# A chunked recurrence with its inverses folded into the chunk matrices, two lines of inverses and one bank for a chunk's forms

## The chip, the cores and the metric

The kernel runs on one core of a Trainium2 chip. The metric is the time of one execution in microseconds (us), as the device measures it. A core has TensorE (matrix products), VectorE, ScalarE, GpSimd (elementwise work), SyncE (here it only starts transfers), an on-chip memory of 128 partitions and, for products, eight banks of accumulators with 512 fp32 columns each. Each engine takes its instructions in the order in which they were written; semaphores order the engines among each other. In the profile, PE is TensorE, DVE VectorE, ACT ScalarE, POOL GpSimd.

## The reference, cut to what matters

A two layer trunk on 1024 prompt frames and 8 streams of 16 sample frames, model width 1024, fp32. Layer 0 mixes tokens by a gated delta rule with 16 heads of 64, layer 1 by banded attention; each is followed by a SwiGLU block. The change touches the delta rule alone:

```python
def step(S, inp):
    r_t, w_t, k_t, v_t, na_t, b_t = inp
    sa = jnp.einsum('bhvk,bhk->bhv', S, na_t)
    S = S * w_t[:, :, None, :] + sa[..., None] * b_t[:, :, None, :] + v_t[..., None] * k_t[:, :, None, :]
    return S, jnp.einsum('bhvk,bhk->bhv', S, r_t)
s_final, out = lax.scan(step, s0.astype(f32), xs)
```

`S` is a head's 64 x 64 state. `na_t` is the negative normalised key, `b_t` that key times a gate, `w_t` the decay. Before it stand projections, decays and a key norm; behind it a norm of each head's output, a bonus term, a gate and the output projection.

## The kernel before, in words

The recurrence is a phase of its own, `recurrence_phase`. It treats the heads two at a time: `PAIRS` = 8 head pairs, one head in partitions 0 to 63, the other in 64 to 127. Time is cut into 18 chunks of 64 frames: 16 of the prompt, one after the other, and two that hold four sample streams each.

Within a chunk the rule is solved in matrix form. `form` computes the chunk's products of decayed keys, queries and values (the *forms*); masks make them triangular. The matrix `I - AB` of the chunk is inverted by doubling blocks: `x0` and `init` set up X and its transpose Y, and each of `LEVELS` levels has two half turns (`invert` with half 0 and 1), Q = L X and then X += Y Q, Y += Q Y. A *step* passes the state through a chunk: w = values + A S, then u = Y w, then S = decay (S + B u + K V), with the outputs beside it. So each of 16 steps goes three times from TensorE to VectorE and back: w (copy L1770), u (copy L1775), state (L1783). Every chunk's step needs the state of the one before.

Two helpers issue every such product as two 64 x 64 products, one for each head: `heads` (line 1309) reads and writes the same half of the partitions, `cross` (line 1315) writes the other half:

```python
def heads(out, lhsT, rhs, start=True, stop=True):
    for lo, hi in halves:
        last = pe.matmul(out[lo:hi], lhsT[lo:hi], ...)
def cross(out, lhsT, rhs, start=True, stop=True):
    for (lo, hi), (to, end) in zip(halves, halves[::-1]):
        last = pe.matmul(out[to:end], lhsT[lo:hi], ...)
```

The banks are FORM_D, FORM_C (forms by heads and by cross), MX, MY (inverses), WU, SB, OB (w and u, state, outputs) and one piece bank, which all other products of the phase share in turn.

What the order is: the work is a list of items for all engines, and each engine walks through it and does its part of each item. `PATTERN`, a string written by hand, merges five threads for each pair: A the serial steps of this pair, B forms, C the preparation of the next pair (sigmoids, the decay scan L1685 with a subtraction behind it, exponentials, key norm by `ksum` and `kexp`, `write`, bonus product), D the finish of the previous pair (`center`, `vsum`, `affine`, `gate`), E the inverses. Chunks are inverted in groups (`GROUPS`), all chunks of a group in one half turn. `stream` puts filler products where TensorE would stand idle, in the first pair's preparation and in the last pair.

## Time and profile before

| | |
|---|---|
| time, median of 3 runs | 3544.43 us (3542.29 to 3555.04) |
| profiled execution: span | 3544.3 us |
| profiled execution: time beside the span | 3544.3 us, core 0, the only core |
| TensorE busy | 3356.9 us, 95% |
| VectorE, ScalarE, GpSimd busy | 1734.0, 1350.6, 1688.5 us |
| mean granted TensorE clock | 0.990 of full |
| recurrence phase | about 411 to 1132 us |

Busy time is the union of an engine's instructions. A matmul's record spans its passage through the array, while the next one starts long before its end, so that a busy TensorE may still be waiting. An fp32 product leaves two records for each half, so a `heads` or a `cross` leaves four.

### The profile page before, as it was taken

What the parts mean: (1) busy time and instruction counts of PE and PEld (TensorE: products, weight loads), DVE (VectorE), ACT (ScalarE), POOL (GpSimd) and SP (SyncE); (2) the same over time, 40 slices, a digit from 0 to 9 for tenths busy, and PEclk for the clock granted to TensorE, in tenths of its full rate; (3) what the DMA queues carried; (4) which work ended last, traced back from release to release, by engine and by line L of the source; (5) the groups of instructions that cost most, each with busy time, mean ns of one, the idle gap of its engine ahead of it and who ended that gap; (6) DMA issues with size and microseconds to landing.
All of it is one profiled execution on the core that took longest, in us unless ns stands there. A gap on an engine that the chain in (4) does not pass through costs nothing. (4 is left out here: it accounts for less than half of the span.)

```text
span 3544.3 us, 86456 instructions
## 1 busy us (share of the span) xinstructions
PE 3356.9 (95%) x32975; PEld 2903.7 (82%) x32975; DVE 1734.0 (49%) x3390; ACT 1350.6 (38%) x2904; POOL 1688.5 (48%) x1513
## 2 busy tenths in 40 slices
PE   8999878888888999999999999999989999999999
PEld 7999767777776988888888887777769988888887
DVE  7113456777665374444444533333343744444444
ACT  6212444445543133333333434444453333333335
POOL 5434345555554445454554544344433354545455
PEclk9999999999999999999999999999999999999999
DMA  4422201111113111111111234544442111111111
GB/s 154 154 88 89 73 24 31 46 39 42 45 54 120 27 43 44 48 45 47 44 45 44 92 85 96 117 98 91 106 108 66 41 46 47 44 49 43 46 44 73
DMA packets 432738, 233.79 MB, mean 66 GB/s; under 512 B 190979, under 2 KB 417043, under 8 KB 431558
## 3 DMA queue, kind: packets, MB, share of 16 engines
q1 hardware_dynamic: 428882, 215.40, 21.7%
q10 hardware_dynamic: 3572, 14.33, 1.0%
q8 instruction: 211, 3.46, 0.4%
q14 instruction: 73, 0.60, 0.0%
HBM read 187.69 MB, written 47.21 MB: 66 GB/s over the span
## 5 line engine op out<-in xcount | busy, mean ns | idle before, releaser
L2615 DVE TENSOR_TENSOR H<-ps,H 128x512 f32<-128x512 f32 x608 | 419.3, 690 | 464.3 <-PE ps L2278 463.5
L2166 POOL TENSOR_TENSOR split<-work,split 128x512 fp32r<-128x512 f32 x280 | 379.5, 1361 | 495.0 <-ACT split L2437 487.9
L2278 PE MATMUL ps<-split,split 128*128 128x512 f32 x1824 | 514.0, 390 | 0.0
L2331 PE MATMUL ps<-xs,split 128*128 128x512 f32 x1920 | 512.5, 393 | 0.0
L1315 PE MATMUL ps<-arena 64*64 64x64 f32 (+2 forms) x8800 | 423.9, 236 | 50.1 <-DVE arena L1770 14.6
L2331 PEld LDWEIGHTS ps<-xs,split 128*128 128x128 f32 x1920 | 349.9, 188 | 68.1
L2278 PEld LDWEIGHTS ps<-split,split 128*128 128x128 f32 x1824 | 339.9, 188 | 70.9 <-DVE H L2615 0.7
L1315 PEld LDWEIGHTS ps<-arena 64*64 64x64 f32 x8800 | 319.7, 136 | 87.5 <-issue 38.2
L2331 PE MATMUL ps<-split,split 128*128 128x512 f32 x1440 | 366.1, 390 | 0.5 <-issue 0.5
L3205 PE MATMUL ps<-xs,split 128*128 128x384 f32 x1656 | 361.2, 355 | 2.6 <-POOL split L3119 2.6
L600 PE MATMUL ps<-mixed,wsplit_mix 128*128 128x384 f32 x1872 | 331.7, 339 | 7.6 <-DVE mixed L823 7.6
L600 PEld LDWEIGHTS ps<-mixed,wsplit_mix 128*128 128x128 f32 x1872 | 330.1, 189 | 8.9 <-DVE mixed L823 8.9
L1309 PE MATMUL ps<-arena 64*64 64x64 f32 (+2 forms) x5632 | 304.4, 241 | 27.4 <-DVE arena L1775 13.2
L2331 PEld LDWEIGHTS ps<-split,split 128*128 128x128 f32 x1440 | 267.6, 188 | 55.5 <-issue 1.0
L3205 PEld LDWEIGHTS ps<-xs,split 128*128 128x128 f32 x1656 | 277.9, 189 | 30.1 <-issue 22.4
L1309 PEld LDWEIGHTS ps<-arena 64*64 64x64 f32 x5632 | 245.8, 135 | 60.7 <-DVE arena L1775 27.3
L2437 ACT CAST split<-work 128x512 fp32r<-128x512 f32 x280 | 174.1, 622 | 138.1 <-PE ps L2331 107.7
L2171 POOL TENSOR_TENSOR split<-work,split 128x256 fp32r<-128x256 f32 x168 | 132.7, 790 | 172.9 <-ACT split L2444 170.3
L3368 ACT ACTIVATE work<-work,work 128x640 f32<-128x640 f32 (+3 forms) x144 | 101.0, 702 | 257.3 <-DVE work L3459 249.3
L3171 POOL TENSOR_SCALAR work<-work,work 128x640 f32<-128x640 f32 (+2 forms) x64 | 95.0, 1484 | 188.7 <-DVE work L3464 188.7
L1284 POOL TENSOR_TENSOR arena<-arena 128x320 f32<-128x320 f32 (+2 forms) x144 | 123.6, 866 | 127.0 <-PE ps L1315 100.0
L2475 ACT COPY ps<-ps 128x512 f32<-128x512 f32 x120 | 68.8, 574 | 281.0 <-PE ps L2331 281.0
(328 smaller groups left out, 5875.4 us busy)
## 6 DMA issues: line engine op xcount, KB each, us to landing
work<-in_ffn_w_gu SPq DMA_DIRECT2D x168, 256.0 KB, 2.9
work<-in_ffn_w_down SPq DMA_DIRECT2D x168, 128.0 KB, 2.4
...
work<-in_cache_k SPq DMA_DIRECT2D x256, 64.0 KB, 2.2
...
```

The lines of the kernel that those rows point to most:

```text
L600: last = pe.matmul(mem.ps[:, 4 * v + c, 0:CW], mem.wsplit[:, v, w, k * P:(k + 1) * P], mixed[part][:, k, c * CW:(c + 1) * CW], start=(k == ...
L1284: pool.tensor_tensor(m.lt[:, n % 2, 0:G, :], m.at[:, slot_of(pr, g), 0:G, 0:64], spread(m.level[:, l, :], G), ALU.mult).then_inc(lt_ready, 1)
L1309: last = pe.matmul(out[lo:hi], lhsT[lo:hi], rhs[lo:hi] if rhs is not None else eye(lo, hi), start=start, stop=stop)
L1315: last = pe.matmul(out[to:end], lhsT[lo:hi], rhs[lo:hi] if rhs is not None else eye(lo, hi), start=start, stop=stop)
L2166: pool.tensor_tensor(w[1], frm, w[0].bitcast(F32), ALU.subtract).then_inc(u_lo, 1)
L2171: pool.tensor_tensor(w[1], mem.down_raw, w[0].bitcast(F32), ALU.subtract).then_inc(d_lo, 1)
L2278: last = pe.matmul(full(DOWN + j % 2), w[part][:, (m % 2) * P:(m % 2 + 1) * P], mem.hid[xpart][:, SEG[h]], start=(a == 0), stop=(a == 2))
L2331: last = pe.matmul(full(to), unit(i)[part][:, k * P:(k + 1) * P], operand[xpart][:, k, :], start=(first and k == 0 and a == 0), stop=(k == ...
L2437: act.copy(w[0], w[2] if i == 3 else mem.raw[:, RAW_OF[i], :]).then_inc(u_hi, 1)
L2615: dve.tensor_tensor(at, full(DOWN + j % 2), at, ALU.add).then_inc(added, 1)
L3205: last = pe.matmul(ps[:, GEMM + b, 0:CW], mem.wsplit[:, (3 * p + u) % 2, w, k * P:(k + 1) * P], mem.xs[:, part, k, c * CW:(c + 1) * CW], s ...
L3368: act.activation(pr, pr, ACT.Exp, scale=-1.0, bias=mem.mx[:, N % 2, h:h + 1], accum_out=mem.rsum[:, N % 2, h:h + 1]).then_inc(ex_ready, 1)
```

## The change

The inverse no longer acts on w within a step. Once a group's inverse is done, a new item `fold` multiplies it into two of the chunk's forms (BR, which gives outputs, and BT, which gives the state's update), so that a step has two turns: w, and the state. For that, Y starts from the transposed form instead of being turned by a product (`init` goes, `x0` on GpSimd sets up both), and X and Y lie side by side so that VectorE adds to both by one operation. All products of the inverses are `heads` now. The forms of a chunk lie in one bank, 512 columns, all by `cross`; two such banks alternate, VectorE masks 320 columns in one operation and ScalarE copies 192. Groups are four chunks each, in two independent lines (threads E and F), each with a bank. Outputs are collected eight chunks at a time. The order has a new string for the start and a new pattern. The filler products in the last pair's steps go. Lines of the changed kernel: `heads` is 1311, `cross` 1317.

```diff
-GROUPS = [(0, 5), (5, 5), (10, 6), (16, 2)]
+GROUPS = [(0, 4), (4, 4), (8, 4), (12, 4), (16, 2)]
+ROUNDS = [(0, 8), (8, 8), (16, 2)]
...
-LEVELS = [5, 5, 5, 3]
-NL = sum(LEVELS)
+LEVELS = [5, 5, 5, 5, 3]
+LINE = [0, 1, 0, 1, 0]
...
-PATTERN = ("EABACDEAAEACAEABECBAEDBAECABAEDAEBCEACEACAEAACAAEECAEDEABEADAECACEACACABEADECAEADECAEAACEDEAEBAEABAEABAEABEAEA"
-           "BACEADEAECADAEACEACAAABAEAAEABCAABAAEAAECCBEAEBAECA")
...
+FIRST = (
+    "CCCCCCCCCCCCCCCCCCCCCEBBBBBBBBEBEBEFFEFEFCEBFEBFEBFEBFEBFEBFFCFC")
+PATTERN = (
+    "DEAEACCFABEAFCEAFACECAFEADAFCAECAFCCDEFADCCEDFCADECAFEADFAABAECFCACDEACDEACBEABCEFABEABEACAEBCAEBACBAEBCAEBAEA"
+    "DEFAFAABEABFEABFEAABFEBAAFAEAFAEAFCEBFEAAFAFABF")
...
-        out += [("x0", o, g), ("init", o, g)] + [("invert", o, (g, l, half)) for l in range(1, LEVELS[g] + 1) for half in range(2)]
...
+            out += [("x0", o, g)] + [("invert", o, (g, l, half)) for l in range(1, LEVELS[g] + 1) for half in range(2)] + [("fold", o, g)]
...
-        FORM_D, FORM_C, MX, MY, WU, SB, OB, PIECE = range(8)
+        FORM, M, WU, SB, OB, PIECE = (0, 1), (2, 3), 4, 5, 6, 7
...
+                    for a, part in enumerate((AB, BA)):
+                        chain.link(pool.tensor_tensor(xy[:, :, a, :], m.slots[:, c0:c0 + G, part], spread(m.level[:, 0, :], G), ALU.mult))
+                    pool.tensor_tensor(xy.rearrange("p q a c -> p (q a) c"), xy.rearrange("p q a c -> p (q a) c"), spread(m.eye, 2 * G), ALU.add).then_inc(x_ready[line], 1)
...
-                    heads(fd[:, 0:192], m.bb[:, e, n, :], m.ar[:, e, n, :])
-                    cross(fc[:, 0:192], m.kb[:, e, n, :], m.ar[:, e, n, :])
-                    heads(fd[:, 192:256], m.ar[:, e, n, 64:128], m.bb[:, e, n, :]).then_inc(formed_d, 1)
-                    cross(fc[:, 192:256], m.vb[:, e, n, :], None).then_inc(formed, 1)
...
+                    fb = bank[:, FORM[now % 2], :]
+                    cross(fb[:, 0:128], m.kb[:, e, n, :], m.ar[:, e, n, :])
+                    cross(fb[:, AB], m.ar[:, e, n, 0:64], m.bb[:, e, n, :])
+                    cross(fb[:, 192:320], m.bb[:, e, n, :], m.ar[:, e, n, :])
+                    cross(fb[:, BT], m.bb[:, e, n, :], None)
+                    cross(fb[:, KT], m.kb[:, e, n, :], None)
+                    cross(fb[:, VT], m.vb[:, e, n, :], None).then_inc(formed, 1)
...
-                            last = cross(bank[:, MX, q * 64:(q + 1) * 64], m.lt[:, n % 2, q, :], m.x[:, q, :])
...
+                            last = heads(mb[:, q * 64:(q + 1) * 64], m.lt[:, line, n % 2, q, :], xy[:, q, 0:64])
...
+                            last = heads(mb[:, q * 128:q * 128 + 64], xy[:, q, 64:128], qs[:, q, :])
                             if l < LEVELS[g]:
-                                last = cross(bank[:, MX, q * 64:(q + 1) * 64], m.y[:, gb, q, :], m.q[:, q, :])
-                                if q == G - 1:
-                                    last.then_inc(m2_done, 1)
-                            last = heads(bank[:, MY, q * 64:(q + 1) * 64], m.q[:, q, :], m.y[:, gb, q, :])
-                        last.then_inc(m3_done, 1)
+                                last = heads(mb[:, q * 128 + 64:q * 128 + 128], qs[:, q, :], xy[:, q, 64:128])
+                        last.then_inc(m2_done[line], 1)
...
+                    for q in range(G):
+                        last = heads(bank[:, M[line], q * 128:(q + 1) * 128], m.xy[:, line, q, 0:64], m.slots[:, c0 + q, 256:384])
...
-                            cross(bank[:, WU, 0:64], m.ar[:, e, n, 64:128], S, False, True).then_inc(w_done, 1)
-                            state_values(pr, g, q)
-                    elif part == 1:
-                        if q == 0:
-                            outs(pr, g, 0)
+                            cross(bank[:, WU, 0:64], m.ar[:, e, n, 0:64], m.s[:, n % 2, :], False, True).then_inc(w_done, 1)
+                            state_values(n)
+                            if not first_out(n):
+                                read(pr, n)
+                    else:
+                        if n == GROUPS[g][0]:
+                            pe.wait_ge(fold_ready[LINE[g]], folds_before(pr, g) + 1)
                         pe.wait_ge(w_ready, now + 1)
-                        if q == 0:
-                            pe.wait_ge(y_ready, turns_before(pr, g) + LEVELS[g] + 1)
-                        cross(bank[:, WU, 64:128], m.y[:, gb, q, :], m.w).then_inc(u_done, 1)
-                        if q + 1 < G:
-                            outs(pr, *after)
-                    else:
-                        pe.wait_ge(u_ready, now + 1)
-                        ob = bank[:, OB, q * 64:(q + 1) * 64]
-                        pe.wait_ge(state_values_done, 16 * pr + n + 1)
-                        heads(bank[:, SB, 0:64], tm[:, 0:64], m.u, False, True).then_inc(s_done, 1)
-                        pe.wait_ge(outs_done, now + (2 if q + 1 < G else 1))
-                        last = cross(ob, m.u, at[:, 64:128], False, False)
+                        cross(bank[:, SB, 0:64], m.slots[:, n, BT], m.w, False, True).then_inc(s_done, 1)
+                        if first_out(n):
+                            outs(pr, n)
+                            if n:
+                                read(pr, n)
                         if n:
-                            last = cross(ob, S, m.ar[:, e, n, 128:192], False, q == G - 1)
-                        last.then_inc(serial_done, 1)
-                        w_values(pr, *after)
+                            pe.wait_ge(read_done, 15 * pr + n)
+                        heads(out_of(n), m.w, m.slots[:, n, BR], False, last_out(n)).then_inc(serial_done, 1)
+                        w_values(pr, n + 1)
+                        if not last_out(n):
+                            outs(pr, n + 1)
...
-                    act.copy(tm[:, 64:192].rearrange("p (x c) -> p x c", c=64),
-                             bank[:, FORM_C, 0:256].rearrange("p (x c) -> p x c", c=64)[:, 0:4:3, :]).then_inc(tmc_ready, 1)
-                    act.wait_ge(atd_ready, now + 1)
-                    act.copy(tm[:, 0:64], bank[:, FORM_D, 0:64]).then_inc(tm_ready, 1)
+                    act.wait_ge(at_ready, now + 1)
+                    act.copy(m.slots[:, n, 320:512], bank[:, FORM[now % 2], 320:512]).then_inc(tm_ready, 1)
...
+                    act.copy(m.slots[:, c0:c0 + G, 256:384], bank[:, M[line], 0:G * 128].rearrange("p (q c) -> p q c", q=G)).then_inc(fold_ready[line], 1)
...
-                    dve.tensor_tensor(at[:, 0:192], bank[:, FORM_D, 64:256], mask[:, 0:192], ALU.mult).then_inc(atd_ready, 1)
-                    dve.wait_ge(tmc_ready, now + 1)
-                    dve.tensor_tensor(at[:, 192:320], bank[:, FORM_C, 64:192], mask[:, 192:320], ALU.mult).then_inc(at_ready, 1)
...
+                    dve.tensor_tensor(m.slots[:, n, 0:320], bank[:, FORM[now % 2], 0:320], mask, ALU.mult).then_inc(at_ready, 1)
...
-                        dve.tensor_tensor(m.x[:, 0:G, :], wide(MX), m.x[:, 0:G, :], ALU.add).then_inc(x_ready, 1)
-                    dve.wait_ge(m3_done, n + 1)
-                    dve.wait_ge(y_ready, turns_before(pr, g) + l)
-                    dve.tensor_tensor(m.y[:, gb, 0:G, :], wide(MY), m.y[:, gb, 0:G, :], ALU.add).then_inc(y_ready, 1)
...
+                    dve.tensor_tensor(xy, bank[:, M[line], 0:G * 128].rearrange("p (q c) -> p q c", q=G)[:, :, 0:xy.shape[2]], xy, ALU.add).then_inc(x_ready[line], 1)
...
-                        dve.tensor_copy(m.u, bank[:, WU, 64:128]).then_inc(u_ready, 1)
+                        dve.tensor_copy(m.w, bank[:, WU, 0:64]).then_inc(w_ready, 1)
...
-            STREAMED_LAST = {("sw", 0): 2, ("su", 0): 2, ("sw", 1): 2, ("su", 1): 2, ("center", 0): 3, ("ns", 1): 4, ("vsum", None): 4}
+            STREAMED_LAST = {("center", 0): 3, ("ns", 1): 4, ("vsum", None): 4}
...
-                    stream(2 if what == "step" and arg[0] == NG - 2 and arg[1] >= 3 else STREAMED_LAST.get((what, arg), 0))
+                    stream(STREAMED_LAST.get((what, arg), 0))
```

How the instructions move, in TensorE's order. First two pieces of one pair's stretch before: head sums (L1321), a second half turn of a group of six where every other product is a `cross` (L1315) and a `heads` (L1309), and a chunk's forms with 192 and 64 columns.

```order
L1321 MATMUL ps<-headones,arena 128x56 x9
L1315 MATMUL ps<-arena 64x64 x2
L1309 MATMUL ps<-arena 64x64 x2
L1315 MATMUL ps<-arena 64x64 x2
L1309 MATMUL ps<-arena 64x64 x2
...
L1309 MATMUL ps<-arena 64x192 x2
L1315 MATMUL ps<-arena 64x192 x2
L1309 MATMUL ps<-arena 64x64 x2
L1315 MATMUL ps<-ident,arena 64x64 x2
```

The same kind of place after: a stretch behind the head sums, with half turns that are `heads` (L1311) alone, sixteen and thirty in a row, then a chunk's forms by `cross` (L1317) alone, and a fold of 128 columns for four chunks.

```order
L1323 MATMUL ps<-headones,arena 128x56 x9
L1330 MATMUL ps<-ident,arena 128x128 x3
L1311 MATMUL ps<-arena 64x64 x16
L1330 MATMUL ps<-ident,arena 128x128 x3
...
L1317 MATMUL ps<-arena 64x128 x2
L1317 MATMUL ps<-arena 64x64 x2
L1317 MATMUL ps<-arena 64x128 x2
L1317 MATMUL ps<-ident,arena 64x64 x6
L1311 MATMUL ps<-arena 64x128 x8
```

The pairs of the two kinds no longer alternate, neither in the inverses nor in the forms. Second, VectorE before, around the decay scan (L1685, printed as the operation that carries it) of one pair: copies of w and u (L1770, L1775), the state (L1783), sums of the inverses (L1757, L1760), masks (L1745, L1747).

```order
L1775 COPY arena<-ps 128x64
L1783 SCALAR_TENSOR_TENSOR arena<-ps,arena 128x64
L1685 SCALAR_TENSOR_TENSOR arena<-arena 128x1152
L1687 TENSOR_TENSOR arena<-arena 128x1152
L1770 COPY arena<-ps 128x64
L1721 TENSOR_SCALAR arena<-ps 128x18
L1723 RECIPROCAL arena<-arena 128x18
L1757 TENSOR_TENSOR arena<-ps,arena 128x384
L1760 TENSOR_TENSOR arena<-ps,arena 128x384
L1775 COPY arena<-ps 128x64
```

And after, the same place: scan (L1670), one sum for X and Y (L1733), the w copy (L1743) and the state (L1751), the key norm (L1679) and the finish of the previous pair (L1705 to L1712).

```order
L1743 COPY arena<-ps 128x64
L1674 TENSOR_SCALAR arena<-ps 128x18
L1676 RECIPROCAL arena<-arena 128x18
L1670 SCALAR_TENSOR_TENSOR arena<-arena 128x1152
L1672 TENSOR_TENSOR arena<-arena 128x1152
L1733 TENSOR_TENSOR arena<-ps,arena 128x512
L1751 SCALAR_TENSOR_TENSOR arena<-ps,arena 128x64
L1705 TENSOR_SCALAR arena<-ps 128x18
L1707 RECIPROCAL arena<-arena 128x18
L1679 SCALAR_TENSOR_TENSOR arena<-arena,vec,ps 128x384
L1733 TENSOR_TENSOR arena<-ps,arena 128x512
```

A sum of an inverse and the state's update now stand behind the scan where a w copy stood; between two of a step's operations there is a sum of the inverses more often than not.

## Rows read from the trace of the kernel before

**Rows 1.** The page: span, busy time, and VectorE's costliest group.

```profile
span 3544.3 us, 86456 instructions
PE 3356.9 (95%) x32975; PEld 2903.7 (82%) x32975; DVE 1734.0 (49%) x3390; ACT 1350.6 (38%) x2904; POOL 1688.5 (48%) x1513
...
L2615 DVE TENSOR_TENSOR H<-ps,H 128x512 f32<-128x512 f32 x608 | 419.3, 690 | 464.3 <-PE ps L2278 463.5
```

**Rows 2.** Windows of the phase, cut at decay scans; busy us of each engine.

```profile
core 0: us, PE busy (x) PEld busy (x) DVE busy (x) ACT busy (x) POOL busy (x), PEclk, DMA share, GB/s
...
448.00:499.50 51.50, 39.75 (x1070) 34.32 (x1069) 21.48 (x68) 19.73 (x58) 21.61 (x27) 0.83 0.09 26
499.50:581.00 81.50, 66.78 (x2091) 57.09 (x2091) 51.57 (x146) 38.97 (x104) 43.27 (x48) 0.96 0.12 33
581.00:905.00 324.00, 287.74 (x8472) 239.92 (x8472) 230.49 (x617) 160.45 (x420) 176.90 (x188) 1.00 0.15 42
905.00:988.30 83.30, 72.64 (x2118) 60.45 (x2118) 57.18 (x154) 40.12 (x105) 44.20 (x47) 1.00 0.14 41
988.30:1132.00 143.70, 124.36 (x3189) 98.06 (x3187) 89.64 (x236) 59.65 (x146) 61.69 (x62) 0.99 0.19 61
```

**Rows 3.** Timeline of TensorE: start, duration of the run, records.

```profile
581.39 0.90 PE L1315 MATMUL ps<-ident,arena 64*64 64x64 f32 x24
```

**Rows 4.** The same timeline, a second half turn of six chunks.

```profile
585.52 0.23 PE L1315 MATMUL ps<-arena 64*64 64x64 f32 x2
585.54 0.23 PE L1309 MATMUL ps<-arena 64*64 64x64 f32 x2
...
585.99 0.22 PE L1315 MATMUL ps<-arena 64*64 64x64 f32 x2
586.00 0.23 PE L1309 MATMUL ps<-arena 64*64 64x64 f32 x2
```

**Rows 5.** Groups by line, 581 to 905 us: TensorE's 64-column products, idle before, releasers.

```profile
L1315 PE MATMUL ps<-arena 64*64 64x64 f32 x3904 | 167.3, 223 | 21.8 <-DVE arena L1770 7.8 <-DVE arena L1757 3.7 <-issue 3.4
...
L1309 PE MATMUL ps<-arena 64*64 64x64 f32 x2496 | 124.2, 225 | 9.3 <-DVE arena L1775 6.2 <-ACT arena L1622 2.9
```

**Rows 6.** Timeline of TensorE at the forms of a chunk.

```profile
623.47 0.38 PE L1315 MATMUL ps<-arena 64*64 64x192 f32 x2
...
623.55 0.36 PE L1309 MATMUL ps<-arena 64*64 64x192 f32 x2
```

**Rows 7.** Groups by line and shape, 581 to 905 us: busy, mean ns of one, idle before.

```profile
L1745 DVE TENSOR_TENSOR arena<-ps,arena 128x192 f32<-128x192 f32 x72 | 25.6, 355 | 20.7 <-PE ps L1309 18.9
...
L1747 DVE TENSOR_TENSOR arena<-ps,arena 128x128 f32<-128x128 f32 x72 | 20.8, 289 | 2.5 <-ACT arena L1614 1.5
...
L1622 ACT COPY arena<-ps 128x320 f32<-128x320 f32 x40 | 17.1, 427 | 23.1 <-PE ps L1315 22.1
L1783 DVE SCALAR_TENSOR_TENSOR arena<-ps,arena 128x64 f32<-128x64 f32 x60 | 16.7, 279 | 10.0 <-PE ps L1309 9.0 <-DVE arena L1732 0.9
L1757 DVE TENSOR_TENSOR arena<-ps,arena 128x320 f32<-128x320 f32 x32 | 15.6, 488 | 7.0 <-PE ps L1315 7.0
...
L1770 DVE COPY arena<-ps 128x64 f32<-128x64 f32 x64 | 14.0, 219 | 11.4 <-PE ps L1315 9.7 <-PE ps L1309 1.2
...
L1605 ACT ACTIVATE arena<-ps 128x384 f32<-128x384 f32 x12 | 5.8, 487 | 7.6 <-PE ps L1315 7.6
...
L1598 ACT ACT_TABLE_LOAD x4 | 5.1, 1283 | 10.0 <-DVE arena L1691 10.0
...
L1598 ACT ACTIVATE arena<-arena 128x1152 f32<-128x1152 f32 x4 | 4.6, 1162 | 0.0
```

**Rows 8.** Timeline of VectorE at the decay scan of a pair.

```profile
581.68 2.55 DVE L1685 TENSOR_TENSOR_SCAN arena<-arena 128x1152 f32<-128x1152 f32 x1
584.26 1.97 DVE L1687 TENSOR_TENSOR arena<-arena 128x1152 f32<-128x1152 f32 x1
```

**Rows 9.** Timeline of VectorE at the first two chunks' forms.

```profile
449.46 0.36 DVE L1745 TENSOR_TENSOR arena<-ps,arena 128x192 f32<-128x192 f32 x1 [0.21 <-DVE arena L1716]
...
451.43 0.36 DVE L1745 TENSOR_TENSOR arena<-ps,arena 128x192 f32<-128x192 f32 x1 [1.41 <-PE ps L1309]
```

369 lines of the change are left out of this document (163 added, 206 removed).

## The prediction

> **What bounds the kernel now.** I read the page's shares and busy digits first, then the windows of the recurrence phase, then TensorE's pace inside it, then who ends its waits. The page gives TensorE 95% of a span of 3544.3 us and the others at most 49% [rows 1]; outside the recurrence the change touches nothing, so 3544.3 minus that phase stays as it is. The profiled execution's span is 3544.3 us and the median of the three runs 3544.43 us, so the sum is made against either.
>
> The windows cut the phase, 411 to 1132 us, at the decay scans of its eight head pairs, one a pair. Four periods from the scan at 581 to that at 905 take 324 us, 81.0 us each, with TensorE shown busy for 287.7 of it, 71.9 a period, VectorE 57.6, ScalarE 40, GpSimd 44 [rows 2]. No engine but TensorE is near full, and TensorE shows 9 us of idle in a period. That understates it. A product's record is shown for 0.22 us, while the next may start in the same place 0.058 us later (below), so each turn that TensorE waits for hides some 0.16 us of waiting under the last record before it. With some 55 such turns in a period that is 9 us more. So I count 18 us of waiting and 63 us of product issue.
>
> The pace matters most here. Each logical fp32 product of 64 columns leaves two records. Where cross products stand alone, 24 records take 0.90 us including the 0.22 us tail: 28 ns a record, 0.117 us for a cross (two halves, four records) [rows 3]. In a half turn of the inverses, where cross and heads alternate, L1315 pairs start at 585.52 and, eight pairs on, at 585.99: steps of 0.059 us, each with two cross and two heads records: 0.117 us for a cross and a heads together [rows 4]. So alternation makes the second product free. The Trainium skill (TensorEngine Tiling (Array Packing), Key Properties) says that the four 64x64 tiles work independently; the heads products use two of them and the cross products the other two. The trace agrees with it: 0.059 us for four records against 0.117.
>
> TensorE's own waits name VectorE's copies L1770 and L1775 (w and u of a step), its sum L1757 and ScalarE's copy L1622 (both of the inverses) [rows 5]. These are turns that the change removes, or puts more work behind.
>
> **The change part by part**, for one period; a unit is 0.117 us, 64 columns by one kind of product.
>
> *Forms, 18 a period.* Before, heads and cross of 192 and of 64 columns overlap: 4 units (a heads of 192 starts 0.08 us after a cross of 192 [rows 6]). After, all eight blocks go by cross into one bank: 8 units. Added 18 x 4 x 0.117 = 8.4 us.
>
> *Inverses.* The first half turns cost 86 units before and after (16 chunks by 5 levels, 2 by 3). The second half turns but the last have 16 x 4 + 2 x 2 = 68 chunk levels; each had cross and heads overlapped (1 unit), now two heads (2 units): added 8.0 us. The turned start (18 units) goes, the fold (18 x 2 units) comes: added 2.1 us.
>
> *Steps.* The u product goes: 8 products a step become 7, minus 16 units. But before, seven of eight stood so that a heads lay beside a cross, and now three heads follow each other (output, next w, next output): I count about 105 units of issue before and 113 after. Added 0.9 us.
>
> *Seams.* Where a cross item stands beside a heads item, one unit overlaps. The new order has about 40 such seams more than counted above: minus 4.7 us. The rest of a period (gates, sums, root expansions, samples: about 20 us) is the same work. Sum: 8.4 + 8.0 + 2.1 + 0.9 - 4.7 = 14.7 us; issue rises from 63 to 77.7 us, and the whole phase's by about 117 us.
>
> *What comes back is waiting.* A turn of a step is the product's 0.22 us, 0.05 to VectorE, 0.21 for the copy and 0.05 back: 0.53 us, and 0.60 us with the state's 0.28 us operation [rows 7]. There were three turns for each of 16 steps and now two. In the new order each of the two has an inverse half turn or more behind it (0.47 us for 4 chunks, 0.94 us for a second half), plus 0.3 us of the step's own products, so nearly all are covered. The inverses ran in one line: 18 levels of about 3.2 us (two half turns of 0.7 us, copy 0.43, sum 0.49, four handovers [rows 7]) plus starts, 70 of 81 us, nearly a bound of its own. Two lines have 13 and 10 levels of the same length, 42 and 32 us: no bound. Forms had one pair of banks, and VectorE's 0.36 and 0.29 us with a copy of ScalarE between stood between two of them; now two banks alternate.
>
> *What remains.* VectorE saves 355 + 289 ns against about 490 ns (the 320-wide sum) for each form, 2.8 us, and the u copies, 3.7 us, and about 1 us in the inverses (a 512-wide sum is 0.69 us by the page's L2615 [rows 1], where there were two of about 0.48). It is not the bound, so this pays only through waits. But its long operations stay in one queue: scan 2.55, subtraction 1.97 [rows 8]. At the scan, the new order puts center, two inverse halves and a step after the head sums, and the second head sums must wait for ScalarE's root of the first (table load 1.28 and 1.16 us [rows 7]) and then center's two reads, the square 0.49 us and a copy as long: those end about 6.1 us after the first sums start, and TensorE has 4.3 us of work. 1.9 us of wait. The expansions behind them alternate in one bank: 0.6. Later halves stand behind ScalarE's exponentials: 0.5. The 1152-wide product for the bonus (as long as the subtraction, 1.97) and the gates: 1. The other places: 2. Sum about 6 us a period. Below, 2 us (the piled work hides all but the scan); above, 12 us, two thirds of what there is now. I take 6, the places counted.
>
> So a period comes to 77.7 + 6 = 83.7 us, 2.7 more than 81.0, and over the six periods from the scan at 499.5 to that at 988.3: the first has less to do (no finish of a pair before it) and idles most now (66.8 busy of 81.5 [rows 2]): 8 us less issue than the others, so 69.5 + 7 of waits = 76.5, minus 5; the other five, now 81.5 on average (407.3 for five [rows 2]), plus 11.5.
>
> *The ends.* 448 to 499.5 us: the first forms are now 2.0 us apart (449.46, 451.43 [rows 9]), waiting on that chain; with two banks they come at about 1.06. Issue there is 44 us after, plus 4 of waits: 48 against 51.5, minus 3.5. The tail, 988.3 to 1132 us, takes 143.7 us for 106 us of issue, 38 us of waiting, the last steps having nothing behind them. After, 120.5 us of issue; 5 us of waits up to its steps, 4 in them (two turns instead of three), 7 in the finish: 137, minus 7. The removed filler products (26 in the last pair) are issued where TensorE waits anyway and count nothing; were that cover gone, each costs 0.15 us, 4 us in all. The copy of the identity blocks at the start, one VectorE instruction, likewise.
>
> Sum: -5 + 11.5 - 3.5 - 7 = -4 us: 3540 us.
>
> The rows of VectorE show a fixed part: 64 wide 0.22, 192 wide 0.36 us [rows 7]. The Trainium skill (VectorE: DVE Perf Modes, The TRN2 errata) says that such operations pay a fixed extra time each, so that fewer and longer ones are cheaper; by it alone VectorE's 7.5 us a period would come off. The trace puts VectorE 23 us from full.
>
> **The rivals.**
> - *Faster: the waits all but vanish.* If only 2 us stay in a period, it is 79.7 us: 4 us less in six periods, and about 3 less at the ends: 3540 - 27 = 3513 us. For it: every turn named in [rows 5] gets more work behind it. Against: VectorE's long operations stay. It holds from waits under about 3.5 us. Chance 0.28.
> - *Slower: the in-order queues keep TensorE waiting while the products cost more.* Place: from the scan to the fold some 20 us later, where ScalarE holds two roots, a table load and three exponentials, each about as long as a root, in front of an inverse's copy, and VectorE the 4.5 us of the scan. If 11 us of waits stay, a period is 88.7: 5 us more by 6, and 2 at the ends: 3572 us. It decides from 9 us on. Against: both lines have work, so one may be late. Chance 0.28.
> - *Faster still: VectorE's saved time comes off in full,* as if its fixed cost for each operation bounded the phase: 8 x 7.5 = 60 us, 3484 us. Against it: VectorE's 23 us of idle in a period [rows 2]. Chance 0.02.
> - *The change does not do what it says:* the two turn step gains nothing, since steps were covered already and only forms and inverses gave waits. Then 2 more turns' waits stay, 3 us a period: 3558 us. This is inside my case; the same chance covers it.
>
> **How the numbers follow.** No change: 0.42, faster 0.30 (0.28 and 0.02), slower 0.28, where 0.5% (18 us) is about what a measurement of this kernel can tell from no change. The range leaves out the 0.02 and the ends: 3505 us is waits of 2 us with issue 1 us a period lower than counted, 3588 us is waits of 12 us (3578) with seams that give 1.2 us less in each of eight periods.
>
> **What would show it.** Right: TensorE's busy share in a period rises from 0.89 to 0.93 or more, while its products' issue takes 77 us; four steady scans stand 83 to 84 us apart; hardly any wait of TensorE ends with the w copy or the state's update; VectorE falls to about 50 us a period; the tail is 7 us shorter. Wrong: if heads alone run at 0.058 us, the added 14.7 us is not there and the kernel gains over 100 us; if scans stand 88 us apart, the queues hold it.

## The result, and the profile after

The changed kernel takes 3584.95 us (median of 4 runs, 3578.57 to 3595.91), the kernel before 3546.06 us, measured beside it (3542.29 to 3555.04): ratio 1.0114, 95% interval 1.009 to 1.0138. It is slower, by 39 us, where I forecast 3540 us and most likely no change. The time lies in my range (3505 to 3588 us), near its upper end, where I had put the rival with the in-order queues. The profiled execution has a span of 3594.0 us, 49.7 more than before. It is the longest of the four runs (3595.91 us), 11 us above the median, so a period read from it may be up to 1.5 us longer than usual; its mean granted clock, 0.982, is also the lowest of the four (the others have 0.984 to 0.987). Where that matters I give the medians' figure too.

The page of the changed kernel, to be held against [rows 1]: TensorE is busy for 91 us more, VectorE for 41 us less, and the span is longer. The two costliest groups of this phase are both products of 64 columns.

```profile
span 3594.0 us, 87138 instructions
...
PE 3448.1 (96%) x33525; PEld 3010.3 (84%) x33525; DVE 1693.0 (47%) x3045; ACT 1338.1 (37%) x2800; POOL 1759.1 (49%) x1633
...
q8 instruction: 214, 3.51, 0.4%
...
L1311 PE MATMUL ps<-arena 64*64 64x64 f32 (+1 forms) x9984 | 400.0, 228 | 17.8 <-issue 10.2
...
L1317 PE MATMUL ps<-arena 64*64 64x64 f32 (+4 forms) x4448 | 287.9, 252 | 14.4 <-DVE arena L1743 5.5
```

The windows of the phase in the changed kernel, cut at its decay scans as in [rows 2]; the columns are the length, then each engine's busy time with its instructions, the granted clock of TensorE, the DMA share and GB/s.

```profile
core 0: us, PE busy (x) PEld busy (x) DVE busy (x) ACT busy (x) POOL busy (x), PEclk, DMA share, GB/s
...
446.00:502.20 56.20, 50.23 (x1374) 45.60 (x1376) 28.43 (x57) 19.03 (x48) 36.65 (x48) 1.00 0.09 24
502.20:584.90 82.70, 74.15 (x2143) 67.75 (x2141) 46.76 (x101) 36.59 (x89) 52.89 (x62) 0.96 0.12 33
584.90:673.90 89.00, 83.04 (x2194) 73.03 (x2198) 52.73 (x113) 38.59 (x92) 53.15 (x62) 0.96 0.13 38
...
855.20:944.10 88.90, 83.21 (x2194) 73.34 (x2194) 52.66 (x113) 38.58 (x92) 53.08 (x62) 0.96 0.13 38
944.10:1033.00 88.90, 83.06 (x2194) 73.16 (x2195) 52.30 (x112) 38.52 (x92) 53.22 (x62) 0.96 0.13 38
```

The steady scans stand 89 us apart and not 81, and TensorE is busy for 0.93 of a period, where it was 0.89: busier, and later. By the scans of both traces: from the first scan to the second 68.6 us against 71.5, the first period 82.7 against 80.9, the next five together 448.1 against 407.5, the tail from the last scan to the end of the phase's products 143.6 against 142.5. So +40.6 of the 49.7 us lie in the five steady periods. The rest is -2.9, +1.8 and +1.1 us, and 9 us outside (the first scan 4.4 us later, the program behind the phase 4.8 us longer), which scatters between executions.

Which waits of TensorE are left, the list of waits from the scan at 673.9 to that at 1033.0 (four periods): in total, times, longest.

```profile
engine line waited for: us in total, times, longest us
PE ps L1323 <- ACT arena L1598: 6.5, 4, 1.6
PE ps L1311 <- issue: 6.2, 8, 1.7
PE ps L1317 <- DVE arena L1743: 2.5, 9, 0.4
PE ps L1317 <- DVE arena L1674: 1.4, 5, 0.3
PE ps L1311 <- DVE arena L1762: 1.3, 4, 0.4
```

The turns of the steps that ended TensorE's waits in [rows 5] have all but gone (L1743, the w copy, 0.6 us a period). The wait before the second head sums is there as forecast, 1.6 us by this list once a period, behind center's read L1598. The second row is what I had not thought of: TensorE stands and waits for nothing that the profile shows.

**Two ledgers.** To compare kernels I split a period in two. I added up, from the start times of TensorE's records over the last four periods, how far each start lies beyond the pace of the record before it (0.058 us for 64 columns, in proportion for more, 0.115 for a full-array product; only where it is more than 0.06 us beyond). "Gaps" are these sums a period, split by what the trace says ended them: a semaphore; the switch between full-array and quarter tiles; nothing, over or under 0.3 us. "Products" is the rest of the period, so a product that the half clock stretches (below) is mostly counted there. By it the 18 + 63 us of the prediction are 17.0 + 64.6.

```
kernel               period  products  gaps | semaphore  switch  nothing, long  nothing, short
before                81.5     64.6    17.0 |   11.9       1.7       1.6            1.8
both taken apart      82.8     68.6    14.2 |   10.2       1.7       1.0            1.3
before + products     90.3     71.1    19.3 |   11.7       5.0       1.1            1.5
before + cover        84.4     67.7    16.8 |   10.4       1.7       3.0            1.6
before, waits once    80.9     63.9    17.0 |   11.7       1.7       1.8            1.8
after                 89.8     75.4    14.4 |    7.1       1.7       2.5            3.1
after + filler        86.9     75.6    11.2 |    6.3       1.3       1.8            1.8
after, merged         89.2     69.9    19.3 |   10.5       1.7       3.7            3.4
after + products      97.1     82.7    14.4 |    7.2       4.8       0.1            2.3
after, slow copy      89.5     75.3    14.2 |    7.0       1.8       2.4            3.0
after, split          92.3     80.1    12.2 |    7.5       1.3       1.4            2.0
after + 216 waits     95.0     76.9    18.1 |    7.0       1.7       5.6            3.7
after without y       83.6     67.8    15.8 |    9.2       1.8       1.9            2.8
after, waits once     85.1     73.3    11.7 |    7.7       1.4       0.5            2.1
  with the filler    84.9     74.3    10.6 |    6.7       1.3       0.9            1.8
```

### The profile page after: what moved, and what is told of

It is laid out like the page before. It is cut to its first block and busy times, and to the rows that moved or that the text cites. A ratio compares the mean times of both kernels' runs of the same rounds, so it can differ in the third digit from the quotient of the medians.

```text
span 3594.0 us, 87138 instructions
## 1 busy us (share of the span) xinstructions
PE 3448.1 (96%) x33525; PEld 3010.3 (84%) x33525; DVE 1693.0 (47%) x3045; ACT 1338.1 (37%) x2800; POOL 1759.1 (49%) x1633
## 3 DMA queue, kind: packets, MB, share of 16 engines
q10 hardware_dynamic: 3572, 14.33, 1.0%
q8 instruction: 214, 3.51, 0.4%
## 5 line engine op out<-in xcount | busy, mean ns | idle before, releaser
L1311 PE MATMUL ps<-arena 64*64 64x64 f32 (+1 forms) x9984 | 400.0, 228 | 17.8 <-issue 10.2
L1311 PEld LDWEIGHTS ps<-arena 64*64 64x64 f32 x9984 | 351.8, 137 | 46.9 <-issue 31.2
L1317 PE MATMUL ps<-arena 64*64 64x64 f32 (+4 forms) x4448 | 287.9, 252 | 14.4 <-DVE arena L1743 5.5
L1317 PEld LDWEIGHTS ps<-arena 64*64 64x64 f32 x4448 | 198.6, 135 | 46.1 <-issue 21.0
L95 POOL TENSOR_SCALAR wsplit_mix<-stage_mix 128x1024 fp32r<-128x1024 f32 x26 | 76.1, 2926 | 202.6 <-PE ps L601 171.4
L2438 ACT COPY ps<-ps 128x512 f32<-128x512 f32 x120 | 68.8, 573 | 280.9 <-PE ps L2294 280.9
```

Of the source, the lines that this page charges most:

```text
L1311: last = pe.matmul(out[lo:hi], lhsT[lo:hi], rhs[lo:hi] if rhs is not None else eye(lo, hi), start=start, stop=stop)
L1317: last = pe.matmul(out[to:end], lhsT[lo:hi], rhs[lo:hi] if rhs is not None else eye(lo, hi), start=start, stop=stop)
```

## The experiments

Ratios are to the kernel before, with their 95% interval.

### Is the pace of alternated products what it was priced at?

**e1_turns_apart**: the kernel before, with the second half turn's cross products all ahead of its heads.

```
                         for q in range(G):
                             if l < LEVELS[g]:
                                 last = cross(bank[:, MX, ...], m.y[:, gb, q, :], m.q[:, q, :])
                                 ...
+                        for q in range(G):
                             last = heads(bank[:, MY, ...], m.q[:, q, :], m.y[:, gb, q, :])
```

> The kernel before with one edit: in a second half turn all cross products come first and all heads products after them, instead of one after the other. Same work, same waits. If products of one kind alone take 0.117 us for 64 columns and alternated ones 0.117 us for both (the pace theory), 68 chunk levels a period get 0.117 us longer, 8.0 us, 64 us over eight pairs, of which waits take up to a third: 3585 to 3610 us. If the kinds do not matter, or waits alone set the period (the queue theory), 3545 us, within 8.

3554.77 us, 1.0014 (1.0001 to 1.0026): between the two expectations.

**e2_forms_apart**: the kernel before, with the forms in the order heads, heads, cross, cross.

```
-                    cross(fc[:, 0:192], m.kb[:, e, n, :], m.ar[:, e, n, :])
                     heads(fd[:, 192:256], m.ar[:, e, n, 64:128], m.bb[:, e, n, :]).then_inc(formed_d, 1)
+                    cross(fc[:, 0:192], m.kb[:, e, n, :], m.ar[:, e, n, :])
```

> The kernel before with one edit: a chunk's forms as two heads products and then two cross products, instead of alternated. Pace theory: 4 units of 0.117 us more for each of 18 chunks, 8.4 us a period, 67 us in all, of which the waits between forms take part: 3565 to 3610 us. Queue theory: 3545 us, within 8.

3550.11 us, 1.0007 (0.9995 to 1.0019): no difference, against the pace that I had priced. **e3_both_apart**, both edits:

> The kernel before with both edits. Pace theory: the two add up, 16.4 us of issue a period, about what the change adds (14.7), without its shorter chain: 3620 to 3670 us, slower than the changed kernel's 3585. Queue theory: 3545 us, within 10.

3558.69 us, 1.0029 (1.0012 to 1.0046). In my sum the second half turns taken apart were worth 8.0 us a period and the forms 8.4. The products' ledger rises by 3.7 us in e1, by 0.5 in e2 and by 4.0 in e3: a run of one kind still overlaps the run or the item of the other kind that stands next to it. Gaps fall by 2.8 in e3, so that 1.2 us a period are left, 9 us in all. Both edits also move a semaphore forward (`m2_done` now stands ahead of the heads products, `formed_d` ahead of the first cross), so that VectorE can start earlier; the ratios alone therefore don't price the pace, the ledger does. The other way round, in the changed kernel:

**a3_merged**: a chunk's forms (cross) and the inverse half turn or fold (heads) that stands beside them are issued in turn, in 14 of 18 chunks; **a4_merged_center** is this with a1, below.

```
+                    a, b = form_calls(form[1], form[2]), line_calls(*inv)
+                    ca = cb = 0
+                    while a or b:
+                        if a and (not b or ca <= cb):
+                            cost, call = a.pop(0)
+                            ca += cost
+                        else:
+                            cost, call = b.pop(0)
+                            cb += cost
+                        call()
```

> The changed kernel with one edit on TensorE alone: where a chunk's forms (cross) stand next to a half turn or a fold (heads), 14 of 18 chunks, their products are issued alternately. Same products, same results, other engines as before. Pace theory: 4 to 8 units of 0.117 us overlap each time, 9 to 10 us of issue a period less; part becomes waiting, since each of the two also waits for the other's inputs: 3510 to 3550 us. Queue theory (waits set the period): 3580 us or more.

> Both: products of forms and inverses alternated, and the last center item early. Pace theory with the clock: the gains add, 3470 to 3520 us, faster than both kernels. Queue theory: not faster than the better of the two alone.

3586.01 us, 1.0100 (1.0083 to 1.0117), and 3600.96 us, 1.0146 (1.0129 to 1.0163), where the changed kernel has 1.0114. No gain clear of the scatter, and a4 is slower. The ledger says why: in a3, alternation takes 5.5 us of products off a period, and the gaps take 4.9 back, 3.4 on semaphores and 1.2 as long stalls that end on nothing. So in neither kernel is alternation worth its price in the period.

### The clock and the wait ahead of the head sums

In the profiled execution of the changed kernel the granted clock falls to half for 6.8 us in every period; before it did so in none of the steady ones. Windows of the changed kernel just ahead of a fall, and over it:

```profile
945.40:947.60 2.20, 0.61 (x25) 0.47 (x22) 2.17 (x2) 2.19 (x5) 2.20 (x1) 1.00 0.00 0
948.40:955.20 6.80, 6.53 (x59) 5.58 (x60) 3.35 (x8) 3.67 (x4) 2.98 (x1) 0.50 0.01 2
```

TensorE does next to nothing for 2 us (the wait behind L1598), then issues head sums, and the clock goes from 2.4 to 1.2 GHz 0.8 us after the first of them. The same wait doesn't always bring the fall: b4_after_split and d3_after_once (below) have it in each steady period, 1.83 and 1.74 us long, and their clock falls in only one and two of the last four.

**a1_center_early** reads the centers further ahead, **a2_filler** lets TensorE do filler products there in all pairs but the last.

```
-    "DEAEACCFABEAFCEAFACECAFEADAFCAECAFCCDEFADCCEDFCADECAFEADFAABAECFCACDEACDEACBEABCEFABEABEACAEBCAEBACBAEBCAEBAEA"
+    "DEAEACCFABEAFCEAFACECAFEADAFCAECAFDCCEFADCCEDFCADECAFEADFAABAECFCACDEACDEACBEABCEFABEABEACAEBCAEBACBAEBCAEBAEA"
```

```
+                if pr + 1 < PAIRS:
+                    fill({("vsum", None): 10, ("affine", 0): 3}.get((what, arg), 0))
```

> The changed kernel with one letter moved in its pattern: the last center item of the previous pair stands before the head sums and the scan instead of behind them, so that ScalarE reads it before the root and not after. The wait of TensorE before the second head sums (1.8 us) should go, and with it the drop of the clock: 4 to 5 us a period, 3550 us. Rival: ScalarE's queue holds the next thing instead (a copy of the inverses), the wait moves and the clock still falls: 3575 to 3585 us.

> The changed kernel with 10 filler products ahead of the second head sums and 3 ahead of the first root expansion in all pairs but the last, where TensorE waits; nothing else changes. Clock theory: the trace of the changed kernel shows the half clock for 6.8 us at each pair's scan, where TensorE waited 1.8 us, and none in the steady periods before; with the waits filled the clock stays up and each period is 2.5 to 3.4 us shorter: 3560 to 3568 us. If the drop has another reason (the low width of the head sums), or costs nothing since engines wait there anyway: 3585 us, within 8.

a1: 3590.72 us, 1.0114 (1.0097 to 1.013), periods of 89.6 us: the wait moves to other places, and the clock is still half for 6.0 us a period. a2: 3577.90 us, 1.0089 (1.0069 to 1.0109). First the window over four periods of the changed kernel, then that of a2:

```profile
673.90:1033.00 359.10, 334.26 (x8764) 293.70 (x8765) 210.03 (x445) 154.31 (x368) 212.54 (x248) 0.96 0.13 38
```

```profile
669.40:1017.00 347.60, 328.69 (x8817) 287.90 (x8821) 211.11 (x446) 154.37 (x368) 213.05 (x248) 1.00 0.14 39
```

With the clock held at 1.00, a period is 86.9 us: 2.9 us less in these four periods, of the 8.2 that the change adds. That is the forecast size, but by the medians the filler is worth only 7 us for the whole kernel, 1 us a period, where I expected 17 to 25, and the intervals of the two ratios overlap. The three other executions of the changed kernel had a higher clock than the profiled one already, so they had less to win. At least 5.3 us a period remain.

### What a period is made of: load tests

Is it the sum of the products, or a chain through VectorE, ScalarE and GpSimd? **b1_after_load** and **b2_before_load** put three filler products of 256 bf16 columns ahead of each chunk's forms in the six middle pairs, **b3_after_slow_q** lets ScalarE copy an inverse's first product chunk by chunk, **b4_after_split** halves the transposing products.

```
+                    fill(fb[:, 0:256], 3 if 0 < pr < PAIRS - 1 else 0)
                     cross(fb[:, 0:128], m.kb[:, e, n, :], m.ar[:, e, n, :])
```

```
-                    act.copy(m.q[:, line, 0:G, :], by64(bank[:, M[line], 0:G * 64])).then_inc(q_ready[line], 1)
+                    for q in range(G):
+                        last = act.copy(m.q[:, line, q, :], bank[:, M[line], q * 64:(q + 1) * 64])
+                    last.then_inc(q_ready[line], 1)
```

```
+                for c in (0, 32):
+                    for (lo, hi), (to, end) in zip(halves, halves[::-1]):
+                        last = pe.matmul(out[to:end, c:c + 32], lhsT[lo:hi], mem.ident[lo:hi, lo + c:lo + c + 32], start=True, stop=True)
```

> The changed kernel with three extra 256-column bf16 products of 128 rows ahead of each chunk's forms, in the six middle pairs: 54 products a pair. By the 28 ns that a 64-column record takes when the queue is dense, 256 columns are 0.11 us, so 5.8 us of TensorE work more in each of six periods, 35 us in all. Theory A (TensorE's issue sets the 88.9 us period, the product term of the forecast): periods grow by 5 to 6 us and the median by about 33 us, 3618. Theory B (a chain of waits through VectorE, ScalarE and GpSimd sets it, and TensorE has slack that sits in front of waits): periods grow by less than 3 us, the median under 15 us, below 3600.

> The kernel before with the same 54 extra 256-column products a pair in the six middle pairs (5.8 us a period). With TensorE waiting 16 us a period there, theory B says that most of it is absorbed in front of waits: under 3 us a period, median under 3565. If every product is paid in full, the period grows by 5 to 6 us and the median is about 3583: then even in the kernel before TensorE work adds to the period one for one, although it waits.

> The changed kernel with ScalarE copying the first product of an inverse turn chunk by chunk (four 64-column copies of 0.21 us, 0.86 us, in place of one of 0.37 us): each turn's chain longer by 0.48 us, ScalarE 10 us busier in a period (from 38.5 to 49). Nothing changes for TensorE. Theory A (issue of products): period within 1 us, median within 8 us of the changed kernel's. Theory B (the chain through the turns, queues in order): 13 turns of the longer line by 0.48 us are 6 us a period if that line is the chain, so a period of 92 to 95 and a median of about 3615 to 3630.

> The changed kernel with the three transposing products of a chunk's forms split into two of 32 columns each: the same columns, 6 products and 6 weight loads more a chunk, 216 records a period more on TensorE's queue (4516 to 4732). Theory C (instruction supply, 256 instructions in 3.4 to 4.1 us at least, 13 to 16 ns each, holds TensorE): 3 us a period, about 22 us in all eight, median about 3607. If columns alone count: same as the changed kernel within 5 us. If a record has a least time of its own near 28 ns whatever its width: 108 pairs a period by 28 to 56 ns less the columns saved, also 3 us; the two are told apart by stalls that end on nothing in the trace at each 256th instruction.

b1: 3633.04 us, 1.0236 (1.0216 to 1.0255). b2: 3597.85 us, 1.0129 (1.0112 to 1.0146). b3: 3585.70 us, 1.0091 (1.0073 to 1.0108). b4: 3622.65 us, 1.0205 (1.0186 to 1.0224). b1 and b2 came out above even the expectation that every product is paid, b3 where the theory of issue has it, and b4 15 us above its 3607 us, which had counted the added products and left out their weight loads.

The products are paid in both kernels, and more than in full: 7.3 us a period in the changed kernel and 8.8 in the one before, for 5.8 us of columns. (b2's profiled execution is 6 us above its median; by the medians, over six pairs, it is 8.0 and 7.8.) Timeline of TensorE in b1 at one of the places:

```profile
903.61 0.57 PE L1311 MATMUL ps<-arena 64*64 64x64 f32 x14
904.11 0.50 PE L1373 MATMUL ps<-ones 128*128 128x256 bf16 x3
904.54 0.43 PE L1317 MATMUL ps<-arena 64*64 64x128 f32 x4
```

The last pair of L1311 starts at 903.96, the next product of quarters at 904.54: 0.58 us where 0.058 would do, 0.52 for 0.33 us of columns. The rest is the switch to the full array and back. By the Trainium skill (TensorEngine Tiling (Array Packing), Key Properties) changing the tiling mode drains TensorE; the trace agrees, at 0.19 us for the two changes.

What does not react is as telling. The semaphore gaps stay: 11.9 and 11.7 us before, 7.1 and 7.2 after. They are round trips between items that stand close together in TensorE's order, and work elsewhere in the order covers nothing of them. The long stalls on nothing do react: they go from 2.5 to 0.1 us a period in b1, which the section on waits for nothing explains. And b3's chain, longer by 0.19 us in each of 23 turns (four copies take 0.56 us by the trace, not the 0.86 that I had expected), changes the period by 0.3 us or less. So a chain through the lines of inverses doesn't set it; that theory is out for additions of this size. b4's 216 product records more, with as many weight loads, cost 2.5 us a period: 4.7 us of products, with 2.2 us of gaps gone. But its clock stayed up in three of these four periods (half for 1.7 us a period, against 6.8), which hides part of the cost; by the medians it is 4.7 us. Its stalls on nothing did not grow, so it doesn't tell the supply of instructions from a record's own time.

**c1_before_cover** puts products directly ahead of a wait, **c3_after_no_y** takes products away.

```
+                        cover(q, SB, 64, True)
                         pe.wait_ge(w_ready, now + 1)
```

```
-                            if l < LEVELS[g]:
-                                last = heads(mb[:, q * 128 + 64:q * 128 + 128], qs[:, q, :], xy[:, q, 64:128])
```

> The kernel before with two extra 64-column products of two quadrants each directly ahead of TensorE's wait for the copy of w, in 13 steps of each of the six middle pairs: 0.117 us each, 0.23 us a step, 3.0 us a period, 18 us in all. Where the products stood elsewhere (ahead of the forms) every one was paid in full although TensorE waits 12 us a period on semaphores. If waits are short round trips, each covered only by what stands between its two ends, these products take the place of the wait (0.19 us each, 2.5 us a period): the period grows by less than 1 us and the median by less than 7 us. If waits don't depend on what stands ahead of them (VectorE's own queue sets when the copy comes), 3 us a period and 18 us.

> The changed kernel with the second product of the second half turn left out (the transposed inverse is not carried on; this leaves out part of the computation) and VectorE adding 64 columns a chunk in place of 128. 64 chunk-turns for the four prompt groups and 4 for the samples have it, 68 by 0.117 us = 8.0 us a period. If the sum of products sets the period: 89.6 to about 82, median about 64 us lower (some 3520). If the chain of a line or the waits set it, the period falls by less than 3 us.

c1: 3562.41 us, 1.0043 (1.0029 to 1.0058): periods 2.9 us longer (2.2 by the medians) for 3.0 us of products. The wait did give way, 1.5 us of semaphore gap a period, but 1.4 us came back as long stalls on nothing. Neither expectation held; the next section has the reason. c3 no longer carries the transposed inverse on, so it leaves out part of the computation and only measures what that part costs. 3540.03 us, 0.9974 (0.996 to 0.9987): 6.2 us a period less for 8.0 us of products (7.6 by the ledger, 1.4 given back in gaps); I had expected nearly all of the 8.0 and some 3520 us. The added products are a true cost: without this one part of them the changed kernel's time is 0.3% under the time before.

### Who ends a wait for nothing

The long stalls of TensorE that end on nothing, first in a3_merged, then in c1_before_cover (timeline, the idle time in brackets):

```profile
811.01 0.33 PE L1331 MATMUL ps<-arena 64*64 64x64 f32 x2 [1.25 <-issue]
...
815.11 0.27 PE L1331 MATMUL ps<-arena 64*64 64x64 f32 x2 [0.60 <-issue]
...
819.01 0.27 PE L1331 MATMUL ps<-arena 64*64 64x64 f32 x2 [0.71 <-issue]
```

```profile
736.86 0.32 PE L1315 MATMUL ps<-arena 64*64 64x64 f32 x2 [0.45 <-issue]
...
741.57 0.39 PE L1315 MATMUL ps<-arena 64*64 64x64 f32 x6 [0.81 <-issue]
...
746.33 0.45 PE L1315 MATMUL ps<-arena 64*64 64x64 f32 x9 [0.86 <-issue]
```

They come 3.9 to 4.8 us apart. I counted all records on TensorE's queue from the program's start: products, weight loads, and also the waits, register and branch instructions (with products and weight loads alone the remainders scatter). Of all steps over 0.45 us between two products that end on nothing, in the five periods from the third scan to the eighth, these stand at a record whose number leaves 165 to 167 when divided by 256:

```
before 8 of 8; after 14 of 14; a3_merged 19 of 19; c1_before_cover 23 of 23; a2_filler 14 of 14;
b4_after_split 8 of 8; c3_after_no_y 11 of 11; e3_both_apart 8 of 8; b3_after_slow_q 16 of 16
```

The same place modulo 256 in kernels with different programs: instructions reach TensorE in blocks of 256, and where it runs faster than blocks come, it stands at the block's edge. The queue q8 moves instructions, 16.4 KB a packet (the page of the changed kernel above: 214 packets, 3.51 MB). Its packets over four periods, in the changed kernel and in the one before:

```profile
q8 instruction: 70, 1.15, 1.3%
```

```profile
q8 instruction: 69, 1.13, 1.4%
```

TensorE's queue has 18064 and 17616 records there, which is 70.6 and 68.8 times 256; in b4_after_split and c3_after_no_y, with more and fewer instructions, it is 77 packets for 77.3 blocks and 62 for 62.1. In these four runs no two packets start less than 3.3 us apart, and the 14 stalls of the changed kernel all end 2.1 to 2.8 us after a packet's start. It fits that b1's fillers, long in columns and few in instructions, leave almost none of the long stalls. To measure the supply by itself:

**d1_dense_runs** puts in two long runs of products that wait for nothing, ahead of the second head sums.

```
+                    if pr in (2, 4):
+                        run(*((128, ("heads", "cross")) if pr == 2 else (256, ("heads",))), pb)
```

> The changed kernel with two long runs of 64-column fp32 products that wait for nothing, ahead of the second head sums: in the third pair 128 times heads and cross in turn (512 products), in the fifth pair 256 times heads alone (512 products); each product is two records with their weight loads, 2048 instructions a run. If the array alone sets the pace (0.117 us a step, both kinds in one step): 15 us for the alternated run, 30 us for heads alone. If the supply of instructions in blocks of 256 is a floor of 4.1 to 4.4 us a block (as between the stalls seen), both runs take 33 to 35 us after the first blocks, with stalls at every 256th instruction, and the alternated pace that the forecast priced holds only for as many instructions as are there in advance.

3641.15 us, 1.0256 (1.0238 to 1.0274). Timeline of TensorE at the alternated run, and at that of heads alone:

```profile
764.59 2.98 PE L1375 MATMUL ps<-ident 64*64 64x64 f32 x186 [1.62 <-ACT arena L1608]
768.72 2.10 PE L1375 MATMUL ps<-ident 64*64 64x64 f32 x128 [1.15 <-issue]
772.20 2.10 PE L1375 MATMUL ps<-ident 64*64 64x64 f32 x128 [1.38 <-issue]
775.95 1.26 PE L1375 MATMUL ps<-ident 64*64 64x64 f32 x69 [1.66 <-issue]
...
967.17 30.08 PE L1375 MATMUL ps<-ident 64*64 64x64 f32 x1024 [1.61 <-ACT arena L1608]
```

The alternated run does a block of 128 product records and as many weight loads in 2 us and then stands. From the stall at 768.72 to the one at 791.52 there are six blocks in 22.8 us: 3.80 us a block, 14.8 ns an instruction. The seven packets of q8 in these microseconds are all that the core's transfers show there, 3.5 to 4.0 us apart, and each stall ends 2.2 to 2.6 us after one starts. The run takes 28.1 us, not 15. Its mean granted clock is 0.94, but the clock was low almost only while the sixth block ran (3.33 us instead of 2.10), and the next block still came 3.76 us after it: the clock is not what holds this run. Heads alone takes 29.9 us with no stall, 14.6 ns an instruction: this kind's own pace (0.117 us for four records with four loads) is just what the supply bears. So alternation is worth something in a burst inside a block and almost nothing over a few microseconds. My expectation was right in kind for the alternated run, and 8 to 16% too high in its size (4.1 to 4.4 us a block); the stalls that I expected in heads alone aren't there. On the average of a period the supply isn't the bound: 4516 records at 14.8 ns are 67 of the changed kernel's 89.8 us (an estimate from d1's rate), so that it costs time only in dense stretches; the long stalls there are 2.5 us.

### Waits that were long fulfilled

**c2_after_waits** adds twelve fulfilled waits ahead of each chunk's forms; **d2_before_once**, **d3_after_once** and **d4_after_once_filler** leave out each wait of TensorE in this phase that an earlier one on its queue already covers, in the kernel before, the changed one, and the changed one with a2's filler.

```
+                    for _ in range(12):
+                        pe.wait_ge(consts, 16)
```

```
+    def wait_ge(self, sem, value):
+        if self.seen.get(id(sem), 0) < value:
+            self.seen[id(sem)] = value
+            self.engine.wait_ge(sem, value)
...
         def _(pe):
+            pe = WaitOnce(pe)
```

> The changed kernel with twelve more semaphore waits that are long fulfilled ahead of each chunk's forms on TensorE's queue: 216 instructions a pair (as many as 108 added products with their weight loads bring in records, half as many as the run with split products), no array work. Instruction supply in blocks of 256 as the cause of stalls that end on nothing: 216 of some 16 ns each, up to 3.5 us a period, median up to 28 us above the changed kernel's. If TensorE's sequencer and the supply have slack except in dense stretches: under 1 us a period, median within 8 us.

> The kernel before, with each of TensorE's semaphore waits in this phase left out where an earlier one on the same semaphore for at least the same value stands on its queue: some 50 waits a pair (the constants' wait ahead of every form and center read, the two for written factors ahead of all but a group's first form). At 24 ns each 1.2 us a period, about 9 us in all, median about 3540 (0.25% faster than the kernel before). If a fulfilled wait costs nothing where TensorE waits 17 us a period anyway: no difference.

> The changed kernel with the same waits left out, some 50 a pair: 1.2 us a period, about 9 us in all: median about 3576 against 3585. If fulfilled waits cost only where twelve stand in a row: no difference.

> The changed kernel with those waits left out and with ten filler products ahead of the second head sums and three ahead of the first expansion of the second roots (the earlier filler run: 7 us). If the two gains add: 3569, still 0.5% slower than the kernel before, since the products that the change adds stay.

c2: 3633.31 us, 1.0245 (1.0223 to 1.0266), +5.2 us a period. Timeline of TensorE: the first form product of each chunk now has idle time before it.

```profile
900.53 0.77 PE L1317 MATMUL ps<-arena 64*64 64x128 f32 x12 [0.27 <-issue]
...
902.49 0.77 PE L1317 MATMUL ps<-arena 64*64 64x128 f32 x12 [0.20 <-issue]
...
905.71 0.77 PE L1317 MATMUL ps<-arena 64*64 64x128 f32 x12 [0.42 <-issue]
```

I had expected 3.5 us at most. By the trace's records the 216 waits a period became 108 instructions of their own (two waits in one), so each costs 48 ns (56 by the medians, over eight pairs). Of the steps over 0.45 us on nothing only 1 of 42 stands at a block's edge: this is not the supply but the queue itself, passing instructions one by one that move nothing.

d2: 3538.99 us, 0.9971 (0.9961 to 0.9981). d3: 3564.04 us, 1.004 (1.0025 to 1.0054). d4: 3562.24 us, 1.004 (1.0025 to 1.0054). The trace shows 65 wait instructions fewer a period in d2 and 77 in d3 (the changed kernel had 136 of its own, before 168). In the kernel before, that gives 0.7 to 0.9 us a period by the trace and 11 us by the medians, 11 to 21 ns each, as expected; d2 beats both kernels. In the changed kernel it gives 4.7 us a period by the trace and 21 us by the medians, twice what I expected. But the clock is in this gain: it is half for 2.5 us a period in d3's trace, where the changed kernel has 6.8, and the 2.1 us of products that go are at least in part that. At the same clock, d4 against a2 (both hold it up), the waits are worth 2.0 us a period by the trace and 16 us by the medians, 25 ns each. The filler adds 2 us more in d4, no longer 7: the two gains are in part the same one. Leaving the waits out also leaves 77 places free in the blocks of instructions, 1.1 us of supply a period by d1's rate; the long stalls on nothing fall from 1.8 to 0.9 us between a2 and d4.

## Why the prediction was wrong, point by point

**The steps that held.** The w copy and the state's update hardly end TensorE's waits any more. The wait before the second head sums is there (1.9 forecast, 1.8 by start times). VectorE falls from 57.6 to 52.5 us a period, and as said nothing follows from it; b3 shows the same for ScalarE. The first forms stand 1.05 us apart on average.

**A hit by luck.** The prologue, scan to scan, is 2.9 us shorter, and 3.5 were forecast. But the forecast was made for the stretch behind the first forms, 48 us against 51.5. From the first mask (449.46 before, 450.81 after) to the second scan it is 51.3 us before and 51.4 after: nothing is gained there, since 45.4 us of products and 7.1 of gaps stand there (from 1 us ahead of the mask) where I had 44 and 4. The 2.9 us lie ahead of the first mask, of which the forecast says nothing.

**The failed step: "I count 18 us of waiting", of which "I take 6" remain.** The 18 us were right as a sum of gaps (17.0), but I took them all for turns that more work can cover. By the trace only 11.9 us end on a semaphore. 5.1 us are switches of the array and stalls on nothing, which the change couldn't remove and in fact raised to 7.3. The semaphore part fell to 7.1, near the 6 that I had counted place by place. So 14.4 us remain and not 6, 8.4 us a period more, and above my upper bound of 12. With the clock held up (a2) it is still 11.2. No kernel of the study comes under 10.6.

**The mis-sized term: the products' 14.7 us.** 10.8 us a period by the ledger, which still has part of the half clock in it. The mechanism is confirmed from both sides: fillers are paid in full, and c3 gives 6.2 of 8.0 us back. But the price rested on [rows 4], an alternated pace seen for 0.5 us. A run of one kind overlaps its neighbours anyway (e1 and e2: 3.7 us for 8.0 and 0.5 for 8.4), so what the change gave up by taking forms and half turns out of alternation was less than I charged. Over several microseconds nothing runs at the alternated pace either (d1); how much of that acts in the short runs of this kernel is not shown. The period's products come to 75.4 us and not 77.7: -2.3 us, which hid part of the first error. Together that is 89.8 for 83.7 us. (Two of the sums are slightly off: 77.7 - 8 is 69.7 and not 69.5, and five periods of 83.7 us are 11.2 us more than 407.3 and not 11.5. Neither matters.)

**The tail and the first period.** I forecast -7 and -5 us; measured are +1.1 and +1.8. Both come from the same step, by the same ledger. The first period has 68.3 us of products and 14.4 of gaps, where I had 69.5 and 7. The tail has 115.5 us of products and 28.1 of gaps (107.9 and 34.6 before), where I had 120.5 and 16: its gaps on semaphores fell from 23.3 to 13.7 us, the others rose from 11.3 to 14.4. Here too my charge for products was too high, and too little waiting went. What ends the tail's waits one by one I did not test.

**The rivals.** The in-order queues (3572 us, "scans stand 88 us apart") had the right period, by a mechanism that is only partly right: their place, from the scan to the fold, holds the 1.8 us wait and what it does to the clock, 7 us by a2's median. The greater part of what could be taken back, 16 us of the median at the same clock (d4 against a2), lies all over the order, in waits long fulfilled. That more waits vanish, and that VectorE's time comes off, are refuted. The Trainium skill's rule that the four tiles work independently (TensorEngine Tiling (Array Packing), Key Properties), which I used for the alternated price, holds within a block of instructions in d1 (128 product records of both kinds in 2.1 us) and is overruled by the supply over several (3.80 us a block).

**What is left open.** d4 (clock mostly held, needless waits out) still has periods of 84.9 us against 80.9 of d2 with the same removal: 4.0 us a period. The products' ledger differs by 10.4 us there, of which 1.4 are the filler, and the gaps by -6.4, so this rest is the added products less the turns saved. I did not try to put the turned products or the fold alone back into the kernel before, so how the 4.0 us split between forms, half turns and fold is not shown. Nor is it shown why a needless wait costs 25 ns in the changed kernel, 11 to 21 in the one before and 48 to 56 in c2; that it stops a queue that would otherwise run ahead of the array is my reading of the gaps that vanish with it, and its place in the blocks of instructions is a rival for part of it. And it is open why the clock fell in each period of one execution and in fewer of others with the same wait.
